# Two-layer transformer and a mixed block on one core: three edits to the order of work around the attention

## The chip, the cores and the metric

The kernel runs on one core of a Trainium2 chip. The metric is device time in microseconds (us) of one execution, the median of several. Engines: PE multiplies matrices, DVE (VectorE) and POOL (GpSimd) do elementwise work, ACT (ScalarE) applies functions and copies, SP issues the DMAs.

## What is computed, cut to what matters

The reference runs a block of two layers on 272 tokens (16 meta tokens and 256 others, 1024 channels), then a second block with routed experts. The change sits in the second layer's attention: 16 query heads of 64 channels, two key/value heads, blocks of 128 queries that see the previous block and their own.

```python
q = (h @ w_q + b_q).reshape(B, L, N_KV_HEADS, GROUP, HEAD_DIM)
...
logits = jnp.einsum('bnqhgd,bnshd->bhgnqs', q, k_blk) * (HEAD_DIM ** -0.5)
logits = jnp.where(valid, logits + bias, -jnp.inf)
m = jnp.maximum(logits.max(axis=-1, keepdims=True), sink)
p = jnp.exp(logits - m)
denom = p.sum(axis=-1, keepdims=True) + jnp.exp(sink - m)
o = jnp.einsum('bhgnqs,bnshd->bnqhgd', (p / denom), v_blk)
return o @ w_o + b_o
```

## The kernel before, in words

Every large matrix product is done in three passes of a reduced format, fp32r, with both factors split into a high and a low part (`mm3`, L1366: high by high, low by high, high by low). A weight piece of 128x2048 comes from HBM into `ring`. ACT makes its high part (`split_hi`, L792), DVE its low part, ring minus high part (`split_lo`, L802); both go to one of four buffer pairs (`wh`/`wl` two of them, `third`, `fourth`). The pieces have one order for the whole program (`NUMBER`), and two counting semaphores, `hi_done` and `lo_done`, say how many are split. `lo_done` is what PE waits for before a product, and what SP waits for before it loads over a ring slot. Four pieces hold w_q (numbers 0 to 3; the key and value weights come between 1 and 2), four hold w_o, then w_gu1 follows.

Each engine runs a program of its own, written out by hand; order within an engine is the order of the code. Around the attention these orders are:

- PE: the products for queries 0 to 3 (a "query" here is a pair of heads, 0 to 7), keys and values; then `scores(0)`, `scores(1)`, `query(4)`, `values()` (three transposes), a wait for `v_ready`; then for u from 0 to 7 `query(5 + u)` (for u below 3), `scores(u + 2)`, for u from 4 the products of w_o's columns 0 and 1 with one pair of heads (`project`), `turn(u)` (transposes of the weights of pair u) and `outputs(u - 1)`. After the loop come the other columns of w_o, c from 0 to 7.
- DVE: `queried(c)` scales a query out of PSUM, `keyed()` the keys (it ends with `kv_ready`, for which `scores(0)` waits), `valued()` the values. `logits(u)` adds the bias and takes the maxima: four instructions that read PSUM and SBUF (L2173), then three on tiles of 128x4 in SBUF (L2181 to L2183), the last of which frees ACT's exponentials. `by_token()` adds the value bias (`v_ready`). `shares(u)` divides: two 128x4 instructions (L2190, L2191) and four on the weights (L2194), for which `turn(u)` waits. `attended_low(u)` (L2199) makes the low part of the output, reading PSUM and SBUF; `project` waits for it. Three low parts of w_o are made by DVE in turns u = 2, 3 and 5.
- ACT: `exps(u + 1)`, `turned(u)` (copies out of PSUM), `attended_high(u - 1)`, and the high parts of w_o: piece 0 ahead of the loop, piece 1 in turn 1, piece 2 in turn 4, piece 3 among the last columns.
- POOL: sums of squares before and after the attention, nothing in between.

`scores(u)` waits for `lg_ready` of `logits(u - 1)`, because the two share PSUM banks. `query(4)` waits for `queried(2)` and `queried(3)`, whose banks it and the next one write over.

Of the kernel before, what the change touches and what calls it, by code (L numbers as in the profile page):

```python
# [5 lines left out]
F32 = mybir.dt.float32  # L6
# [4 lines left out]
ALU = mybir.AluOpType  # L11
# [5 lines left out]
KD = D // P  # L17
# [36 lines left out]
PIECE = 2048  # L54
# [3 lines left out]
FIRST = {}  # L58
# [8 lines left out]
NUMBER = {_piece: _i for _i, _piece in enumerate(SPLIT)}  # L67
FIRST_PIECE = {_name: NUMBER[_name, 0] for _name, _ in SPLIT}
# [84 lines left out]
def bass_two_blocks(nc, a, out):  # L153
# [4 lines left out]
    with ctx:  # L158
# [5 lines left out]
        def sem(name):  # L164
            if name not in sems:
                sems[name] = ctx.enter_context(nc.semaphore(name))
            return sems[name]
# [10 lines left out]
        ring = sb("ring", [P, SLOTS, SLOT])  # L178
# [143 lines left out]
        def tile_at(t):  # L322

            return t % SLOTS, t // SLOTS
# [74 lines left out]
        for part in SPLIT:  # L399
            if part in THIRD:  # L400
                k = 2
            elif part in FOURTH:
                k = 3
            else:
                k, turn_of = turn_of, 1 - turn_of
# [3 lines left out]
        def split_buffer(name, i, j):  # L409

            p = i * 2 + j if type(i) is int else 4 + j
            k = BUFFER[name, p]
            if k >= 2:
                high, low = third if k == 2 else fourth
                return high[:, :], low[:, :]
            return wh[:, k, :], wl[:, k, :]
# [202 lines left out]
        def sum_chunks(pool, name, n):  # L619

            total = sqsum[:, 0:n]
            if SUMMED_BEFORE[name]:
                pool.wait_ge(sem("sq_used"), SUMMED_BEFORE[name])
            pool.wait_ge(sem("sq_ready"), SQ0[name] + 2)
            pool.tensor_tensor(total, square_at(name, 0)[:, 0:n], square_at(name, 1)[:, 0:n], ALU.add).then_inc(sem("sq_summed"), 1)  # L625
            for c in range(2, SUMMED[name]):
                pool.wait_ge(sem("sq_ready"), SQ0[name] + c + 1)
                pool.wait_ge(sem("sq_summed"), sums(name, c - 1))
                pool.tensor_tensor(total, total, square_at(name, c)[:, 0:n], ALU.add).then_inc(sem("sq_summed"), 1)
# [40 lines left out]
            ins.then_inc(sem(done), 1)  # L670


        @block.gpsimd
        def _(pool):
            chain = Chain(pool, "pool_chain")
# [25 lines left out]
            ffn_pool(pool, 0, T)  # L701
            sum_chunks(pool, "ffnpost0", T)
            sum_chunks(pool, "pre1", T)
            sum_chunks(pool, "mixpost1", SEQ)
            sum_chunks(pool, "ffnpre1", SEQ)
            ffn_pool(pool, 1, SEQ)
# [66 lines left out]
            chain(act.activation(r, ps[:, 6, 0:n], ACT.Ln, scale=1.0 / width, bias=EPS))  # L773
            act.activation(r, r, ACT.Exp, scale=-0.5).then_inc(sem("r_ready"), 1)

        def parts_of(name, split, w, size):

            if name != "w_q":
                return [(split[:, 0:size], w)]
            by_pair = split.rearrange("p (k c h n) -> p c k h n", k=KD, h=2, c=2)  # L780
            by_half = w.rearrange("p (k h c n) -> p c k h n", k=KD, h=2, c=2)
            return [(by_pair[:, c], by_half[:, c]) for c in range(2)]

        def split_hi(act, name, slot, rnd, i, j, size):

            if j == 0:
# [4 lines left out]
            for to, src in parts_of(name, high, ring[:, slot, j * size:(j + 1) * size], size):  # L791
                ins = act.activation(to, src, ACT.Copy)  # L792
            ins.then_inc(sem("hi_done"), 1)

        def split_lo(dve, name, slot, rnd, i, j, size):

            piece = NUMBER[name, i * 2 + j] if type(i) is int else i * 2 + (FIRST_PIECE[name] + j)
            dve.wait_ge(sem("hi_done"), piece + 1)
            high, low = split_buffer(name, i, j)
            w = ring[:, slot, j * size:(j + 1) * size]  # L800
            for (to, src), (h, _) in zip(parts_of(name, low, w, size), parts_of(name, high, w, size)):
                ins = dve.tensor_tensor(to, src, h.bitcast(F32), ALU.subtract)  # L802
            ins.then_inc(sem("lo_done"), 1)

        def kv_hi(act):

# [18 lines left out]

        def wo_bank(c):
            return ps[:, (c + 2) % 4, 0:SEQ]

        def halves(name, i, size):
            slot, rnd = tile_at(FIRST[name] + i)  # L830
            return [(slot, rnd, i, j, size) for j in range(2)]

        HEAD_PAIRS = NH // 2

# [505 lines left out]
        def _(pe):  # L1340
# [36 lines left out]
            slot, rnd = tile_at(FIRST["w_pool"])  # L1377
            pe.wait_ge(sem(f"tile_ready{slot}"), 16 * (rnd + 1))
            pw = ring[:, slot, 0:2048].rearrange("p (g k n) -> p g k n", g=4, k=2)
            for c in range(KD):  # L1380
# [4 lines left out]
                for k in range(2):  # L1385
                    ins = mm(ps[:, c % 4, 0:T], pw[:, g, k, c % 2 * P:c % 2 * P + P], pooled[:, 2 * g + k, :],  # L1386
                             start=(k == 0), stop=(k == 1))
# [20 lines left out]
            for c in range(4):  # L1408
                for k in range(KD):
                    pe.wait_ge(sem("x_ready"), KD + k + 1)  # L1410
                    ins = mm(ps[:, c, 0:SEQ], q_weights(c, k)[0], xl[:, k, 0:SEQ], start=False, stop=(k == KD - 1))
# [10 lines left out]
            def query(c):  # L1422

                pe.wait_ge(sem("lo_done"), NUMBER["w_q", c // 2] + 1)
                pe.wait_ge(sem("q_ready"), 4 if c < 6 else c - 1)
                for k in range(KD):
                    ins = mm3(ps[:, 2 + c % 2, 0:SEQ], q_weights(c, k), (xh[:, k, 0:SEQ], xl[:, k, 0:SEQ]), k == 0, k == KD - 1)
                ins.then_inc(sem("q_psum"), 1)
# [9 lines left out]
            def scores(u):  # L1438
                if u >= 4:
                    pe.wait_ge(sem("q_ready"), u + 1)  # L1440
                for j in range(2):
                    rows = slice(j * HD, j * HD + HD)
                    if u:
                        pe.wait_ge(sem("lg_ready"), 4 * (u - 1) + 2 * j + 2)
                    for t in (j, 2 + j):
                        first, n = keys_of(t)
                        ins = mm(score_bank(t)[:, 0:n], qT[rows, u, t // 2 * P:(t // 2 + 1) * P], kT[rows, first:first + n],
                                 start=True, stop=True)
                    ins.then_inc(sem("s_psum"), 1)
# [34 lines left out]

            pe.wait_ge(sem("kv_ready"), 1)
            scores(0)
            scores(1)
            query(4)
            values()
            pe.wait_ge(sem("v_ready"), 2)  # L1490
            for u in range(HEAD_PAIRS):
# [17 lines left out]
            for c in range(4):  # L1509
                for k in range(6, KD):  # L1510
                    ins = project(c, k)
# [3 lines left out]
            for c in range(4, KD):  # L1515
                pe.wait_ge(sem("sq_ready"), SQ0["mixpost1"] + c - 3)
                for k in range(KD):
                    ins = project(c, k)
# [77 lines left out]
            n = Z_HIGH_FIRST  # L1596
# [500 lines left out]
        def _(dve):  # L2097
# [29 lines left out]
            def queried(c):  # L2127

                dve.wait_ge(sem("q_psum"), c + 1)
                chain(dve.tensor_tensor(sq[:, c % 2, 0:SEQ], ps[:, c if c < 4 else 2 + c % 2, 0:SEQ], r[:, N_META:], ALU.mult))  # L2130
                dve.tensor_scalar(qT[:, c, :].rearrange("p (b q) -> p b q", q=P)[:, :, ::-1],
                                  sq[:, c % 2, 0:SEQ].rearrange("p (b q) -> p b q", q=P), query_bias[:, c % 2 * 4 + c // 2:c % 2 * 4 + c // 2 + 1], HD ** -0.5,
                                  ALU.add, ALU.mult).then_inc(sem("q_ready"), 1)

            def keyed():

                dve.wait_ge(sem("kv_psum"), 1)
                chain(dve.tensor_tensor(sq[:, 2, :], ps[:, 4, 0:T], r, ALU.mult))
                dve.tensor_scalar(kT, sq[:, 2, :], key_bias, None, ALU.add).then_inc(sem("kv_ready"), 1)

            def valued():

                dve.wait_ge(sem("kv_psum"), 2)
                dve.tensor_tensor(vT, ps[:, 5, 0:T], r, ALU.mult).then_inc(sem("kv_ready"), 1)

            def by_token():
# [4 lines left out]
                dve.tensor_tensor(vtok[:, 1:NB + 1, :], ps[:, 7, P:3 * P].rearrange("p (b n) -> p b n", b=NB),  # L2151
                                  b_v.unsqueeze(1).to_broadcast([P, NB, P]), ALU.add).then_inc(sem("v_ready"), 1)

            queried(0)
            queried(1)
            split_lo(dve, "w_q", *halves("w_q", 1, PIECE)[0])
            queried(2)
            queried(3)
            keyed()
            split_lo(dve, "w_q", *halves("w_q", 1, PIECE)[1])  # L2160
            dve.wait_ge(sem("tables_loaded"), 64)

            def logits(u):
# [32 lines left out]
            def attended_low(u):  # L2196
                dve.wait_ge(sem("oh_ready"), u + 1)
                o = ps[:, 6 + u % 2, 0:SEQ].rearrange("p (b q) -> p b q", q=P)[:, :, ::-1]
                dve.tensor_tensor(att_l[:, u, :].rearrange("p (b q) -> p b q", q=P), o,  # L2199
                                  att_h[:, u, :].bitcast(F32).rearrange("p (b q) -> p b q", q=P), ALU.subtract)\  # L2200
                   .then_inc(sem("o_ready"), 1)

            logits(0)
            valued()
            logits(1)
            by_token()
            for u in range(HEAD_PAIRS):
                shares(u)
                if u < 4:
                    queried(4 + u)  # L2210
                if u + 2 < HEAD_PAIRS:
                    logits(u + 2)
                if u >= 2:
                    attended_low(u - 2)
                if u in (2, 3, 5):
                    split_lo(dve, "w_o", *[*halves("w_o", 0, PIECE), halves("w_o", 1, PIECE)[0]][(2, 3, 5).index(u)])
            for u in range(HEAD_PAIRS - 2, HEAD_PAIRS):
                attended_low(u)
            split_lo(dve, "w_o", *halves("w_o", 1, PIECE)[1])
            for x in halves("w_gu1", 0, PIECE):  # L2220
                split_lo(dve, "w_gu1", *x)
# [438 lines left out]
```

## Time and profile before

| | |
|---|---|
| runs | 1018.13 us median of 3 (1017.79 to 1020.28) |
| profiled execution | 1017.53 us, its span 1015.8 us |
| busy in the span | PE 94%, DVE 53%, ACT 41%, POOL 20% |
| attention up to the last w_o columns | 257 to 327 us of the span, then PE is busy without a break to 345 |

Times in the trace are from the start of the span. An instruction's row has its start and its duration; a number in brackets is the idle time of the engine before it, and what ended it. The granted clock is a share of PE's full clock of 2.4 GHz; its other level is half of that.

### The profile page before, as it was taken

To read this page: it belongs to the slowest core of one execution; us is meant where nothing else is said; L and a number is where in the kernel's file an instruction comes from. 1 tells how busy PE (TensorE), PEld (TensorE's weight loads), DVE (VectorE), ACT (ScalarE), POOL (GpSimd) and SP (SyncE) were. 2 spreads that over 40 slices of the span, in tenths; PEclk is the share of its full clock that TensorE was granted. 3 is DMA by queue.
4 is the path that set the end of the run, shared out by engine and by line. 5 is a ranking of instruction groups with operands and counts; after the bars stand their busy time and mean duration, and the time that the engine had idled before them with its cause. 6 is when DMAs were issued, how large, how long until landed. Compare 5 with 4: busy or idle time off the path is not lost.

```text
span 1015.8 us, 16586 instructions
## 1 busy us (share of the span) xinstructions
PE 953.5 (94%) x6776; PEld 792.7 (78%) x6776; DVE 537.5 (53%) x931; ACT 415.0 (41%) x691; POOL 202.7 (20%) x261
## 2 busy tenths in 40 slices
PE   4799999999889999999999999988899999999986
PEld 2699999998777899999998999768745545554465
DVE  4765455436966565555448638764632333233266
ACT  4443433435755644344346546743211111111172
POOL 5233333112000433333112412202100000000013
PEclk8799999999998999999999999999899999999998
DMA  7424463448802425533564431118459999999911
GB/s 305 165 85 178 190 227 114 160 164 220 209 31 84 166 85 206 207 139 134 205 226 167 166 127 51 47 54 336 207 216 419 417 420 422 421 422 420 420 66 42
DMA packets 36781, 211.75 MB, mean 208 GB/s; under 512 B 2529, under 2 KB 16113, under 8 KB 17521
## 3 DMA queue, kind: packets, MB, share of 16 engines
q1 hardware_dynamic: 36720, 210.91, 54.5%
q8 instruction: 42, 0.69, 0.3%
q14 instruction: 19, 0.15, 0.0%
HBM read 209.83 MB, written 1.07 MB: 208 GB/s over the span
## 4 chain that ended last, share of the span: by engine, by line
PE 83%; DVE 10%; ACT 3%; POOL 2%; issue 2%; DMA 1%; DVEq 0%; POOLq 0%; ACTq 0%
PE ps L1366 48%; PE ps L1786 11%; PE ps L1800 6%; PE ps L1809 3%; PE ps L1358 2%; DVE mix L1931 2%; PE ps L1758 2%; PE ps L1759 1%; DVE hs L611 1%; PE ps L1293 1%; DVE wl L802 1%; PE ps L1386 1%; PE ps L1301 1%; PE ps L1744 1%; PE ps L1727 1%
## 5 line engine op out<-in xcount | busy, mean ns | idle before, releaser
L802 DVE TENSOR_TENSOR wl<-ring,wh 128x2048 fp32r<-128x2048 f32 (+3 forms) x104 | 205.9, 1981 | 174.6 <-ACT wh L792 174.5
L792 ACT ACTIVATE wh<-ring 128x2048 fp32r<-128x2048 f32 (+3 forms) x104 | 172.3, 1660 | 257.2 <-PE ps L1366 254.9
L1366 PE MATMUL ps<-xh,wh 128*128 128x256 f32 (+3 forms) x600 | 170.0, 283 | 2.3 <-DVE wl L802 1.3
L1366 PE MATMUL ps<-xh,wl 128*128 128x256 f32 (+3 forms) x600 | 168.3, 281 | 0.0
L1366 PE MATMUL ps<-xl,wh 128*128 128x256 f32 (+3 forms) x600 | 168.3, 280 | 0.0
L1366 PEld LDWEIGHTS ps<-xh,wh 128*128 128x128 f32 (+3 forms) x600 | 110.3, 184 | 3.9 <-DVE wl L802 1.5
L1366 PEld LDWEIGHTS ps<-xh,wl 128*128 128x128 f32 (+3 forms) x600 | 110.3, 184 | 0.1
L1366 PEld LDWEIGHTS ps<-xl,wh 128*128 128x128 f32 (+3 forms) x600 | 110.3, 184 | 0.0
L1366 PE MATMUL ps<-acth,wh 128*128 128x272 f32 (+1 forms) x352 | 100.4, 285 | 0.0
L1366 PE MATMUL ps<-acth,wl 128*128 128x272 f32 (+1 forms) x352 | 100.1, 284 | 0.0
L1366 PE MATMUL ps<-actl,wh 128*128 128x272 f32 (+1 forms) x352 | 99.9, 284 | 0.0
L1366 PE MATMUL ps<-xhT,wh 128*128 128x272 f32 x320 | 92.3, 288 | 0.0
L1366 PE MATMUL ps<-xhT,wl 128*128 128x272 f32 x320 | 92.2, 288 | 0.0
L1366 PE MATMUL ps<-xlT,wh 128*128 128x272 f32 x320 | 92.2, 288 | 0.0
L650 POOL TENSOR_TENSOR mix<-mix 128x272 f32<-128x272 f32 (+1 forms) x44 | 36.8, 835 | 156.8 <-DVE mix L1959 141.5
L1366 PEld LDWEIGHTS ps<-acth,wh 128*128 128x128 f32 x352 | 66.4, 189 | 0.0
L2477 DVE TENSOR_TENSOR yl<-ps,yh 128x512 fp32r<-128x512 f32 x32 | 20.6, 686 | 86.3 <-ACT yh L1231 86.3
L1366 PEld LDWEIGHTS ps<-actl,wh 128*128 128x128 f32 x352 | 66.2, 188 | 0.0
L1366 PEld LDWEIGHTS ps<-acth,wl 128*128 128x128 f32 x352 | 66.2, 188 | 0.0
L625 POOL TENSOR_TENSOR sqsum<-mix 128x256 f32<-128x256 f32 (+1 forms) x5 | 4.3, 870 | 280.6 <-ACT mix L767 280.6
L1366 PEld LDWEIGHTS ps<-xhT,wl 128*128 128x128 f32 x320 | 60.3, 188 | 0.0
L1366 PEld LDWEIGHTS ps<-xhT,wh 128*128 128x128 f32 x320 | 60.2, 188 | 0.0
(433 smaller groups left out, 1931.3 us busy)
## 6 DMA issues: line engine op xcount, KB each, us to landing
wring<-in_w_eg SPq DMA_DIRECT2D x32, 2048.0 KB, 13.4
ring<-in_w_gu SPq DMA_DIRECT2D x22, 2048.0 KB, 7.5
wring<-in_w_ed SPq DMA_DIRECT2D x16, 2048.0 KB, 12.0
ring<-in_w_dn SPq DMA_DIRECT2D x16, 1408.0 KB, 6.0
ring<-in_w_z SPq DMA_DIRECT2D x7, 2048.0 KB, 7.7
ring<-in_w_out SPq DMA_DIRECT2D x4, 1152.0 KB, 5.1
ring<-in_w_q SPq DMA_DIRECT2D x8, 512.0 KB, 6.3
ring<-in_w_o SPq DMA_DIRECT2D x8, 512.0 KB, 15.6
```

Of the source, the lines that this page charges most:

```text
L611: eng.tensor_tensor(hs[:, c, cols], hs[:, c, cols], mix[:, c, 0:n], ALU.add).then_inc(hs_add(c), 1)
L650: pool.tensor_tensor(mix[:, 6 + j, 0:n], mix[:, 2 + j, 0:n], mix[:, 4 + j, 0:n], ALU.mult)\
L792: ins = act.activation(to, src, ACT.Copy)
L802: ins = dve.tensor_tensor(to, src, h.bitcast(F32), ALU.subtract)
L1358: mm(ps[:, 6, 0:n], ones[0:rows, :], src, start=first, stop=(c == last)).then_inc(sem("sq_used"), summed if c < summed else 1)
L1366: ins = mm(o, p, q, start=first and n == 0, stop=last and n == 2)
L1758: mm(out, h2h[:, k, at], select[:, k, :], start=(k == 0), stop=False)
L1786: ins = mm(ps[rows, 4, :], x[:, k, rows], chunk(slot)[:, j, i * 512:(i + 1) * 512], start=(k == 0), stop=(k == KD - 1))
L1800: ins = mm(ps[rows, 6 + i, :], heT[:, k, rows], chunk(slot)[:, j, k * D + i * 512:k * D + (i + 1) * 512], start=(k == 0), stop=(k == 1))
L1809: ins = mm(ps[:, c // 2, c % 2 * SEQ:(c % 2 + 1) * SEQ], y[:, c * P:(c + 1) * P], weights, start=False, stop=last and y is parts[-1], skip ...
L1931: return dve.scalar_tensor_tensor(dst, src, V(name, c), r, ALU.mult, ALU.mult)
L2477: dve.tensor_tensor(yl[:, i * 512:(i + 1) * 512], ps[:, 6 + i, :], yh[:, i * 512:(i + 1) * 512].bitcast(F32), ALU.subtract).then_inc(sem(" ...
```

## The change

Three edits. (1) On DVE the low part of w_q's piece 2 moves ahead of `queried(0)`, and `keyed()` ahead of `queried(2)`; the low part of piece 3 moves behind `logits(0)` and `valued()`. (2) On PE `query(4)` moves between `scores(0)` and `scores(1)`. (3) The low parts of w_o's pieces 0, 1 and 2 are made by POOL, which first waits until all pieces before w_o are done; DVE makes that of piece 3 after a wait for POOL's last. `halves`, `parts_of` and `split_lo` move up in the file without a change.

```diff
@@ POOL's program
             sum_chunks(pool, "pre1", T)
+            pool.wait_ge(sem("lo_done"), NUMBER["w_o", 0])
+            for x in [*halves("w_o", 0, PIECE), halves("w_o", 1, PIECE)[0]]:
+                split_lo(pool, "w_o", *x)
             sum_chunks(pool, "mixpost1", SEQ)
@@ PE's program
             pe.wait_ge(sem("kv_ready"), 1)
             scores(0)
+            query(4)
             scores(1)
-            query(4)
             values()
@@ DVE's program
+            split_lo(dve, "w_q", *halves("w_q", 1, PIECE)[0])
             queried(0)
             queried(1)
-            split_lo(dve, "w_q", *halves("w_q", 1, PIECE)[0])
+            keyed()
             queried(2)
             queried(3)
-            keyed()
-            split_lo(dve, "w_q", *halves("w_q", 1, PIECE)[1])
             dve.wait_ge(sem("tables_loaded"), 64)
...
             logits(0)
             valued()
+            split_lo(dve, "w_q", *halves("w_q", 1, PIECE)[1])
             logits(1)
             by_token()
...
                 if u >= 2:
                     attended_low(u - 2)
-                if u in (2, 3, 5):
-                    split_lo(dve, "w_o", *[*halves("w_o", 0, PIECE), halves("w_o", 1, PIECE)[0]][(2, 3, 5).index(u)])
             for u in range(HEAD_PAIRS - 2, HEAD_PAIRS):
                 attended_low(u)
+            dve.wait_ge(sem("lo_done"), NUMBER["w_o", 3])
             split_lo(dve, "w_o", *halves("w_o", 1, PIECE)[1])
```

## Rows read from the trace of the kernel before

**Rows 1.** PE by stretch: us, PE busy (instructions), granted clock, DMA share, GB/s.

```profile
276.80:281.20 4.40, 4.40 (x26) 0.64 0.98 417
299.30:305.30 6.00, 3.78 (x34) 0.88 0.00 0
315.70:321.20 5.50, 3.79 (x25) 0.69 0.00 0
257.00:327.00 70.00, 61.00 (x494) 0.93 0.39 108
```

**Rows 2.** Timeline of PE: start, duration, instruction, idle before it.

```profile
272.40 0.40 PE L1447 MATMUL ps<-work 64*128 64x144 f32 x2 [1.69 <-DVE work L2139]
275.24 0.39 PE L1447 MATMUL ps<-work 64*128 64x144 f32 x1 [1.88 <-DVE small L2173]
282.32 0.39 PE L1366 MATMUL ps<-xh,third_h 128*128 128x256 f32 x1 [0.70 <-DVE work L2151]
285.33 0.95 PE L1447 MATMUL ps<-work 64*128 64x144 f32 x8
302.43 0.33 PE L1459 MATMUL ps<-cst,work 128*128 128x128 f32 x1 [2.22 <-DVE work L2194]
317.41 0.44 PE L1459 MATMUL ps<-cst,work 128*128 128x128 f32 x1 [1.74 <-DVE work L2194]
```

**Rows 3.** Timeline of DVE around the queries, keys and first logits.

```profile
266.36 0.42 DVE L2130 TENSOR_TENSOR sq<-ps,rstd 128x256 f32<-128x256 f32 x1
271.99 0.36 DVE L2139 TENSOR_SCALAR work<-sq,small 128x272 f32<-128x272 f32 x1
275.79 0.17 DVE L2181 TENSOR_TENSOR small<-small,row 128x4 f32<-128x4 f32 x1
276.14 0.43 DVE L2144 TENSOR_TENSOR work<-ps,rstd 128x272 f32<-128x272 f32 x1
```

**Rows 4.** Timeline of DVE, a low part of w_o and what follows.

```profile
299.22 2.28 DVE L802 TENSOR_TENSOR wl<-ring,wh 128x2048 fp32r<-128x2048 f32 x1
301.42 0.16 DVE L2190 TENSOR_TENSOR small<-small 128x4 f32<-128x4 f32 x1
```

**Rows 5.** The page, DMA issues: KB each, us to landing.

```profile
ring<-in_w_gu SPq DMA_DIRECT2D x22, 2048.0 KB, 7.5
```

**Rows 6.** Timeline of POOL after the attention.

```profile
333.82 0.75 POOL L625 TENSOR_TENSOR sqsum<-sq 128x256 f32<-128x256 f32 x1 [76.82 <-ACT sq L767]
```

**Rows 7.** Groups by form on POOL: busy, mean ns; idle before.

```profile
L656 POOL TENSOR_TENSOR actl<-mix,acth 128x272 f32 x22 | 17.1, 775 | 3.7 <-POOL acth L653 3.7
L694 POOL TENSOR_TENSOR sgw<-sgw,cst 128x512 f32<-128x512 f32 x1 | 1.3, 1263 | 9.2 <-DMA sgw<-in_sgw 9.2
```

**Rows 8.** Timelines of POOL and DVE at three places where both work.

```profile
17.40 1.28 POOL L603 TENSOR_TENSOR work<-work 128x512 f32<-128x512 f32 x1
17.47 1.51 DVE L1931 SCALAR_TENSOR_TENSOR work<-hs,vec,rstd 128x272 f32<-128x272 f32 x1
...
565.14 2.29 DVE L802 TENSOR_TENSOR wl<-ring,wh 128x2048 fp32r<-128x2048 f32 x1 [3.46 <-ACT wh L792]
565.45 2.58 POOL L723 TENSOR_TENSOR work<-work,rstd 128x256 f32<-128x256 f32 x1 [9.69 <-ACT work L1033]
...
1003.79 0.72 POOL L641 TENSOR_TENSOR sqsum<-sqsum,sq 128x256 f32<-128x256 f32 x1
1003.84 0.43 DVE L2507 TENSOR_TENSOR mix<-ps,rstd 128x256 f32<-128x256 f32 x1 [0.82 <-PE ps L1366]
```

**Rows 9.** Timeline of DVE, the second row of group 8's kind, undisturbed.

```profile
248.03 0.50 DVE L1931 SCALAR_TENSOR_TENSOR mix<-mix,vec,rstd 128x272 f32<-128x272 f32 x1 [2.15 <-ACT rstd L774]
```

**Rows 10.** Timeline of ACT, two high parts of w_o.

```profile
293.57 1.91 ACT L792 ACTIVATE third_h<-ring 128x2048 fp32r<-128x2048 f32 x1
...
311.26 1.91 ACT L792 ACTIVATE wh<-ring 128x2048 fp32r<-128x2048 f32 x1
```

More of the change, by code:

```diff
@@ L670, in conv, with halves, parts_of, split_lo @@
             ins.then_inc(sem(done), 1)
+        def halves(name, i, size):
+            slot, rnd = tile_at(FIRST[name] + i)
+            return [(slot, rnd, i, j, size) for j in range(2)]
+        def parts_of(name, split, w, size):
+            if name != "w_q":
+                return [(split[:, 0:size], w)]
+            by_pair = split.rearrange("p (k c h n) -> p c k h n", k=KD, h=2, c=2)
+            by_half = w.rearrange("p (k h c n) -> p c k h n", k=KD, h=2, c=2)
+            return [(by_pair[:, c], by_half[:, c]) for c in range(2)]
+        def split_lo(dve, name, slot, rnd, i, j, size):
+            piece = NUMBER[name, i * 2 + j] if type(i) is int else i * 2 + (FIRST_PIECE[name] + j)
+            dve.wait_ge(sem("hi_done"), piece + 1)
+            high, low = split_buffer(name, i, j)
+            w = ring[:, slot, j * size:(j + 1) * size]
+            for (to, src), (h, _) in zip(parts_of(name, low, w, size), parts_of(name, high, w, size)):
+                ins = dve.tensor_tensor(to, src, h.bitcast(F32), ALU.subtract)
+            ins.then_inc(sem("lo_done"), 1)
         @block.gpsimd
@@ L774, in rsqrt @@
             act.activation(r, r, ACT.Exp, scale=-0.5).then_inc(sem("r_ready"), 1)
[L776 to L782, printed above, removed]
         def split_hi(act, name, slot, rnd, i, j, size):
@@ L793, in split_hi @@
             ins.then_inc(sem("hi_done"), 1)
[L795 to L803, printed above, removed]
         def kv_hi(act):
@@ L827, in wo_bank @@
             return ps[:, (c + 2) % 4, 0:SEQ]
-        def halves(name, i, size):
-            slot, rnd = tile_at(FIRST[name] + i)
-            return [(slot, rnd, i, j, size) for j in range(2)]
         HEAD_PAIRS = NH // 2
```

## The prediction

> **What bounds the kernel now.** PE is busy 94% of the span, so I looked for the stretches where it is not. PE's windows show one around the attention: of 70.0 us from 257 to 327 it is busy 61.0, and its granted clock is 0.93 [rows 1]. So 9.0 us are idle time and another 4.9 (70.0 x 0.07) are half-speed time; after 327 PE runs densely again, so whatever reaches the end of `outputs(7)` earlier ends the kernel earlier by as much. Next, PE's own timeline names the stalls [rows 2]: 1.69 us ahead of `scores(0)` (the keys, L2139), 1.88 ahead of `scores(1)` (the end of `logits(0)`'s use of the banks), 0.70 ahead of `query(5)` (`by_token`), 2.22 ahead of `turn(3)` and 1.74 ahead of `turn(6)`, the last two for `shares`. Each is a wait for DVE. The reader is to see that the stalls cost twice: behind the first pair the clock is 0.64 for 4.40 us of `query(4)`, 1.6 us lost; behind the stall of 2.22 it is 0.88 over 6.0 us, 0.7 lost; at `turn(6)` 0.69 over 5.5, 1.7 lost [rows 1]. DVE's timeline then shows what stands ahead of the waits.
>
> **Edit 1, keys earlier.** DVE is free for the queries at 266.36 and done with the keys at 272.35 [rows 3]; in these 6.0 us lie four `queried`, a split (2.2 us, from one start to the next [rows 4]) and `keyed` (0.85), so a `queried` is 0.73. Two of them leave the path: keys at 270.9. The split of w_q's piece 2 stands ahead either way, and its high part comes from ACT's earlier work. PE ends the values' product at 270.71 (272.40 less 1.69), so `scores(0)` goes at 270.95 and ends at 271.9 (0.95 [rows 2]).
>
> **Edit 2, `query(4)` in between.** It needs `queried(3)`, whose end stays at 272.35. It takes 3.0 us at full clock (282.32 to 285.33, `query(5)`) and covers `logits(0)`: PE ends it at 275.35, `scores(1)` at 276.3, the transposes at 276.8. On DVE, without the split of piece 3 (2.2), `logits(0)` ends at 273.95 instead of 276.14 [rows 3]; `valued` 0.35, the split 2.2: DVE turns to `logits(1)` at 276.5. Its four PSUM reads take 1.3 (1.65 in all, less the 0.35 from 275.79 to 276.14 [rows 3]): 277.8. If nothing else came, 0.35 for the small instructions and 0.7 for `by_token` [rows 2] would start `query(5)` at 278.8, 3.5 us earlier than 282.32. The load of w_gu1 over piece 3's slot is issued by SP behind that split, 1.9 us later than now; it lands in 7.5 us [rows 5] and ACT reads it some 50 us later, so it costs nothing.
>
> **Edit 3, low parts by POOL.** POOL has nothing from 257 to 333.82 [rows 6], so its own time is free. DVE loses three splits, 6.6 us. The price of one on POOL is not in the trace: 0.775 us for 272 elements, 1.263 for 512 [rows 7]. The slope gives 0.775 + 1776 x 0.00203 = 4.4 us; in proportion to the smaller one it would be 5.8. I take 4.4, because the two rows show a fixed part; 5.8 is kept as the upper end, and 4.0 as the lower for a slope measured on one instruction. `project` needs piece 0 some 20 us after it is ready and piece 1 and 2 in the columns behind 327, so that POOL is slow costs PE nothing directly.
>
> It costs through DVE. Three places show both at work [rows 8]. A POOL instruction of two SBUF inputs runs 17.40 to 18.68; DVE's L1931 (two SBUF inputs) that starts at 17.47 takes 1.51 instead of 0.50 [rows 9] and ends 0.3 after POOL's. The other way round, POOL's 256 elements that start 0.31 into a split of DVE take 2.58 us and end 0.6 after it. But L2507, which reads PSUM and SBUF, takes 0.43 in the middle of a POOL instruction. So I read: an instruction with two SBUF inputs waits until the other engine's is over, one that reads PSUM doesn't. The Trainium skill ("SBUF — State Buffer", section "Who interferes with whom") states this for any length: the pair of ports is held for the whole instruction, and the second to come fully blocks. The sum below is by whole holds, as the rows of up to 2.3 us show; the first rival is the sum if a hold of 4.4 us doesn't happen. The same skill's "GPSIMD Engine Reference" (section "Performance versus the Vector engine") gives 4497 ns for a two-input operation of 2048 elements, no run here shows it; with it the sum would be 0.3 us higher.
>
> Piece 0: POOL waits for w_q's last split, 276.5, and so starts exactly when DVE turns to `logits(1)`. The four PSUM reads pass, the 128x4 instructions of L2181 to L2183 (two SBUF inputs) meet POOL's hold at 277.8 and wait until 276.6 + 4.4 = 281.0. Behind them on DVE are `by_token` and `shares(0)`; PE waits for the first: 281.0 + 0.35 + 0.7 = 282.05, against 282.32. Of the 3.5 us, 0.3 are left. And PE is now idle in one piece, 276.8 to 282.05, 5.2 us, where before two stalls with 3.6 us were followed by a loss of 1.6. I expect 1.6 to 3.2 lost in `query(5)` and `query(6)`, and take 1.9. Turns 0 to 2, which PE paces, are then 1.6 late (1.9 - 0.3).
>
> Piece 1: ACT makes its high part 1.6 late, 295.2 to 297.1 [rows 10]; POOL holds 297.1 to 301.5. The small instructions of `logits(4)` come inside this and wait; then 0.35, `attended_low` 0.33, and 1.0 of `shares(3)` (301.42 to 302.43 [rows 2, 4]): `turn(3)` at 303.2, 0.8 late. The wait replaces the split.
>
> Piece 2: from `turn(3)` to ACT's next high part are 8.8 us now (302.43 to 311.26 [rows 2, 10]), DVE's second split in them; 2.2 less, 0.3 more where PE becomes the pace: 6.9, so 310.1, ready 312.0. POOL holds to 316.4, and again the small instructions (here of `logits(7)`) come into it; 0.35 + 0.33 + 1.0: `turn(6)` at 318.1 against 317.41. The stall ahead of it is longer than now, the slow clock behind it the same.
>
> **Sum: -0.3 + 1.9 (clock) - 0.8 (turn 3) - 2.0 (turn 4) + 1.9 (turn 6) = +0.7 us.** The profiled execution (1017.53, span 1015.8) would be 1018.2; the median of the runs is 0.6 above it, so 1018.8. Each microsecond on POOL's 4.4 comes three times. Own range: POOL at 4.0 and the clock at 1.6 give -0.8, POOL at 4.8 and 3.2 give +3.2: 1017 to 1021.5.
>
> **Rivals.** (a) DVE isn't held. Then `query(5)` gains 3.5, `turn(3)` its stall of 2.2 and the 0.7 of clock, `turn(4)` 0.6 by the same reckoning, `turn(6)` 1.7 and 1.7: 10.4 us, 1007.7. For it: no row has a hold of 4 us. Against: none of the rows shows a hold end early. 0.13. (b) Only the long ones are held, the 128x4 ones slip through; no row shows one beside a two-input POOL instruction. `query(5)` at -3.5; POOL holds 292.0 to 296.4, `shares(3)` comes at 295.7 and waits 0.7, `turn(3)` at 297.4, -5.0; third high part ready at 305.9, hold to 310.3, `turn(6)` at 311.3: -6.1 us, 1012.0. 0.14. (c) The other side: POOL's price is nearer 5.8. With three times the difference the sum is +4.9, 1023.0; it is slower by over 0.3% from 5.2 us on. For it the proportion, against it the two rows' slope. 0.14. (d) `logits`' reads of PSUM, a custom instruction with its second input in SBUF, are held too: 1.2 us more behind piece 0 and 1.0 more behind piece 1, some of it kept: +2.9, 1021.7. L2507 speaks against it. 0.09. My forecast: 0.50.
>
> **The numbers.** About 0.3%, 3.1 us, is what a measurement of this kernel can tell from no change. Faster: (a), (b): 0.27. Slower: (c) above 5.2 us and a part of (d), 0.18. The rest, 0.55. The range leaves out (a) and the end of (c): 1010.5 to 1022.5.
>
> **What would show it.** `scores(0)` near 271, `query(4)` at a full clock near 272.4; three POOL splits of 4.4 us; at the first, L2181 behind `logits(1)` at 3 us instead of 0.17, ending with POOL's; PE idle near 5 us ahead of `query(5)` and a low clock behind it; `turn(3)` and `turn(6)` each released by a DVE that had waited for POOL. I am wrong if L2181 is short there, if POOL's splits are not near 4.4, or if the clock stays at 1.00 after the long idle time.

## The result, and the profile after

The change makes the kernel slower: 1022.82 us median of 20 runs against 1019.15 (20 runs), ratio 1.0034 (1.0024 to 1.0044), that is 3.5 us. I had said 1018.8 against 1018.13, or +0.7. So 1.0 us of the 4.0 between 1018.8 and 1022.82 is the kernel before, whose median went from 1018.13 (3 runs) to 1019.15. The profiled execution of the change has a span of 1019.5 us, against 1015.8.

PE's timeline of the kernel after: `scores(0)`, `query(4)`, `query(5)`, `turn(3)` and `turn(6)`.

```profile
270.34 0.95 PE L1450 MATMUL ps<-work 64*128 64x144 f32 x8 [0.37 <-DVE work L2142]
271.88 0.35 PE L1369 MATMUL ps<-xh,third_h 128*128 128x256 f32 x1 [0.58 <-DVE work L2134]
281.39 0.58 PE L1369 MATMUL ps<-xh,third_h 128*128 128x256 f32 x1 [5.16 <-DVE work L2154]
302.02 0.33 PE L1462 MATMUL ps<-cst,work 128*128 128x128 f32 x1 [1.45 <-DVE work L2196]
316.72 0.47 PE L1462 MATMUL ps<-cst,work 128*128 128x128 f32 x1 [3.67 <-DVE work L2196]
```

Of the two stalls of 1.69 and 1.88 us, 0.37 ahead of `scores(0)` and 0.58 ahead of `query(4)` are left. `query(4)` starts at 271.88, `query(5)` waits 5.16 us, `turn(3)` 1.45 instead of 2.22, and `turn(6)` 3.67 instead of 1.74.

The timeline of POOL in the kernel after, from its last sum of squares before the attention to the first behind it. I use the distance of the starts of these two rows as the length of the attention in every run below.

```profile
254.32 1.92 POOL L629 TENSOR_TENSOR sqsum<-sqsum,mix 128x272 f32<-128x272 f32 x2 [1.24 <-ACT mix L792]
276.03 4.50 POOL L692 TENSOR_TENSOR wl<-ring,wh 128x2048 fp32r<-128x2048 f32 x1 [19.79 <-DVE wl L692]
295.92 4.54 POOL L692 TENSOR_TENSOR third_l<-ring,third_h 128x2048 fp32r<-128x2048 f32 x1 [15.39 <-ACT third_h L809]
310.63 4.54 POOL L692 TENSOR_TENSOR wl<-ring,wh 128x2048 fp32r<-128x2048 f32 x1 [10.17 <-ACT wh L809]
335.43 0.74 POOL L625 TENSOR_TENSOR sqsum<-sq 128x256 f32<-128x256 f32 x1 [20.26 <-ACT sq L792]
```

It is 81.11 us (335.43 less 254.32); before, 78.74 (333.82 in [rows 6] less 255.08, where the same row stands in the timeline of the kernel before). DVE's timeline of the kernel after shows what each of POOL's three splits does, at the first 128x4 instruction of `logits(1)`, `logits(4)` and `logits(7)` (0.17 us in [rows 3]):

```profile
277.13 3.42 DVE L2183 TENSOR_TENSOR small<-small,row 128x4 f32<-128x4 f32 x1
...
298.44 0.42 DVE L2175 CUSTOM_DVE_ANT_0 work<-ps,work 128x256 f32<-128x256 f32 x1
...
298.90 1.59 DVE L2183 TENSOR_TENSOR small<-small,row 128x4 f32<-128x4 f32 x1
...
310.91 4.28 DVE L2183 TENSOR_TENSOR small<-small,row 128x4 f32<-128x4 f32 x1
```

Each ends where POOL's split ends (276.03 + 4.50 = 280.53; 295.92 + 4.54 = 300.46; 315.17), though it works on four elements per partition. The next one, at 280.58, takes 0.16 again. The row with PSUM as its first input, at 298.44, lies within POOL's second split and takes its usual 0.42.

PE's windows from `turn(6)` to POOL's first sum, in the order: the kernel before, the kernel before in a second profiled execution (a run below), the kernel after, and the kernel after in its second. Columns as in [rows 1].

```profile
317.40:333.80 16.40, 16.39 (x141) 0.90 0.00 1
```

```profile
317.50:332.40 14.90, 14.82 (x141) 1.00 0.00 1
```

```profile
316.70:335.40 18.70, 18.68 (x141) 0.77 0.00 1
```

```profile
316.60:335.30 18.70, 18.67 (x140) 0.77 0.00 1
```

The same work without a break takes 14.9 us at a full clock, 16.4 at 0.90 and 18.7 at 0.77. Up to `turn(6)` the two kernels are equal (62.3 us from the first POOL row before, 62.4 after). What the change adds to the attention comes behind it.

The attention is not the whole difference of the two spans: 3.7 us are 0.8 less ahead of it, 2.4 more in it and 2.1 more behind it, where the code is the same. PE's windows from 700 to 760 us, before and after, show a lower clock there:

```profile
700.00:760.00 60.00, 52.73 (x294) 0.94 0.60 245
```

```profile
700.00:760.00 60.00, 52.90 (x289) 0.89 0.56 228
```

From POOL's sum at 702.70 to the next, at 980.36, are 277.7 us before; in the change 279.9 (704.55 to 984.41). Of the runs below, the second execution of the kernel before, e4 and e9 have 277.6 to 277.7, all others 279.6 to 281.8. Since two variants of the change have the short time and e1 and e6, without POOL, the long one, it doesn't go with the edits. What sets it is open.

### The profile page after: what moved, and what is told of

Read it like the earlier page. It is cut to its first block, busy times and chain, and to the rows that moved or that the text cites. A ratio compares the mean times of both kernels' runs of the same rounds, so it can differ in the third digit from the quotient of the medians.

```text
span 1019.5 us, 16588 instructions
## 1 busy us (share of the span) xinstructions
PE 952.9 (93%) x6776; PEld 791.7 (78%) x6776; DVE 540.2 (53%) x928; ACT 415.7 (41%) x691; POOL 216.8 (21%) x264
## 4 chain that ended last, share of the span: by engine, by line
PE 79%; DVE 13%; ACT 3%; POOL 2%; issue 2%; DMA 1%; POOLq 0%; DVEq 0%; ACTq 0%
PE ps L1369 46%; PE ps L1789 11%; PE ps L1803 6%; PE ps L1812 3%; DVE mix L1934 2%; PE ps L1761 2%; PE ps L1361 2%; DVE hs L611 2%; PE ps L1762 2%; DVE wl L692 1%; DVE small L2183 1%; PE ps L1304 1%; PE ps L1747 1%; DVE work L2175 1%; PE ps L1389 1%
## 5 line engine op out<-in xcount | busy, mean ns | idle before, releaser
L692 DVE TENSOR_TENSOR wl<-ring,wh 128x2048 fp32r<-128x2048 f32 (+3 forms) x102 | 201.5, 1977 | 174.6 <-ACT wh L809 174.5
```

## The experiments

All ran beside the kernel before. "Attention" is the distance defined above, from one profiled execution each; "rest" is what the span has behind it, where no run differs in its code. What lies ahead of the attention takes 254.1 to 255.3 us in every one. A single execution can lie far from the median of its kernel: that of e4 is the fastest of 12 runs (1014.84 us, median 1019.04), that of e8 the slowest of 6 (1026.22, median 1023.02). A difference "by the runs" between two variants is that of their ratios, each known to 1.0 to 3.0 us either way.

| run | ratio to before (interval) | attention | rest |
|---|---|---|---|
| before; again | 1 | 78.7; 77.2 | 682.0; 683.3 |
| change; again | 1.0034 (1.0024 to 1.0044) | 81.1; 81.3 | 684.1; 684.0 |
| e1 edits 1 and 2 alone | 0.9974 (0.9959 to 0.9990) | 75.7 | 686.7 |
| e2 edit 3 alone | 1.0020 (1.0006 to 1.0033) | 81.4 | 684.1 |
| e3 filler at both stalls | 0.9982 (0.9969 to 0.9994) | 76.0 | 686.4 |
| e7 filler at `turn(6)` | 1.0007 (0.9993 to 1.0022) | 77.6 | 684.6 |
| e9 filler at `query(5)` | 1.0012 (0.9996 to 1.0027) | 79.0 | 683.7 |
| e4 first split behind `shares(0)` | 0.9996 (0.9984 to 1.0008) | 75.7 | 682.2 |
| e10 third split behind `shares(7)` | 0.9987 (0.9973 to 1.0001) | 74.8 | 685.2 |
| e8 POOL's splits in halves | 1.0039 (1.0026 to 1.0053) | 81.6 | 688.1 |
| e5 all three where DVE is free of them | 0.9940 (0.9924 to 0.9956) | 69.8 | 689.1 |
| e6 the three on DVE, in its idle times | 0.9902 (0.9872 to 0.9931) | 69.8 | 683.7 |

**e1 and e2: which edit costs.** e1 is the change without its lines on POOL, with DVE's three splits back at u = 2, 3 and 5. e2 has only those lines.

> Edits 1 and 2 alone; DVE makes the three low parts of w_o where it did before. Theory (POOL's splits hold DVE, and the idle time this leaves on PE costs clock): query(5) starts near 278, 3.5 us earlier than before, the four stalls behind it are as before, and so the kernel is 3 to 4 us faster than before, near 0.9965. Rival (the move of query(4) is what costs, since PE has nothing behind it but the wait for the values): PE idle of 4 us or more ahead of query(5) and low clock there with no POOL at work, time 1 to 4 us above before.

> Edit 3 alone. Theory: POOL starts behind w_q's last split, now ahead of logits(0); its three 128x4 instructions are held some 3.4 us, query(4) covers that on PE, and query(5) starts within 0.3 us of before. turn(3) 0.7 earlier, turn(6) 0.7 earlier but behind a longer stall, with up to 2.3 us more at half clock: 0 to +2 us against before. Rival (the three edits do harm only together): 3 us or more faster, since DVE is rid of 6.6 us.

The orders on DVE and PE are worth 2.7 us by the runs (3 to 4 forecast) and 3.0 or 1.5 by the attention, against the first or the second execution of the kernel before; `query(5)` starts at 278.16, behind 1.89 us of idle time, so the rival on edit 2 falls. POOL alone costs 2.0 us, with a stall of 3.66 ahead of `turn(6)` and the clock at 0.77 behind it, as in the change. The rival that edit 3 is good by itself falls too. Its time is at the upper end of the forecast, but the starts that I gave were missed: counted from POOL's last sum, `query(5)` comes 1.3 us later than before (forecast within 0.3), `turn(3)` 0.5 and `turn(6)` 0.3 later (forecast 0.7 earlier each). `scores(1)` takes 2.27 us there instead of 1.62, and in `query(4)` the clock is 0.50 from 277 to 280 us.

**e3, e7, e9: what the idle time costs in clock.** `stay_busy` issues bf16 products whose result nobody reads.

```diff
             values()
+            stay_busy(pe, 4, 21)                  # e3, e9
             pe.wait_ge(sem("v_ready"), 2)
...
+                if u == 6:                        # e3, e7
+                    pe.wait_ge(sem("pt_ready"), 12)
+                    stay_busy(pe, 4, 14)
                 turn(u)
```

> The change, and PE multiplies filler (bf16, 512 columns, nothing is read of it) into free banks during its two long idle times: 21 behind the transposes of the values, 14 ahead of turn(6). Theory (the clock behind the idle times is the part that I sized too small): the granted clock stays 1.00 behind both, 1.4 us come back at query(5) and up to 4 behind turn(6), so the kernel is 4 to 5 us faster than the change and 0 to 2 us faster than before. Rival (the loss lies elsewhere, behind the attention): within 1.5 us of the change.

> The change, with filler on PE ahead of turn(6) only. Theory (my sum left out the longer half-clock time behind the longer stall at turn(6)): the low clock behind query(5) stays, that behind turn(6) goes; 2.5 to 4 us faster than the change, that is 0 to 1 us above before. Rival (the stall ahead of query(5) is the larger part): under 1.5 us faster than the change.

> The change, with filler on PE ahead of query(5) only. The attention is counted from POOL's last sum before it to POOL's first sum after it: 78.7 us before, 81.1 in the change, 76.0 with filler at both places, 77.6 with filler at turn(6) only. Theory (the two low clocks cost independently): 79.3 to 79.9, 1.2 to 1.8 below the change. Rival (the filler only shifts the low clock to a later stretch): within 0.5 of the change's 81.1.

Up to the filler nothing moves: counted from POOL's last sum, `query(5)` starts at 27.1 us in e3 and e9 as in the change, and `turn(6)` at 62.7 in e7, against 62.4. The clock differs, with what follows from it, and the attention falls from 81.2 to 77.6 with filler at `turn(6)`, to 79.0 at `query(5)`, to 76.0 at both: 3.6, 2.2 and 5.2 us. By the runs, the change's 3.5 us become 0.7, 1.2 and -1.8. The 79.0 of e9 is outside the 79.3 to 79.9 that I expected: only 1.3 of its 2.2 us are won ahead of `turn(6)`, the other 0.8 behind it, where the clock is 0.81 over 17.9 us behind the same stall of 3.67. From `turn(6)` on, the run with filler there shows a full clock again:

```profile
317.50:332.20 14.70, 14.70 (x140) 1.00 0.00 1
```

**e4 and e10: one hold at a time.**

```diff
             pool.wait_ge(sem("lo_done"), NUMBER["w_o", 0])
+            pool.wait_ge(sem("p_ready"), 4)                # e4: shares(0) is done
...
+            pool.wait_ge(sem("p_ready"), 4 * HEAD_PAIRS)   # e10, ahead of piece 2: shares(7) is done
```

> The change, with POOL's first split held back until shares(0) is done, so that it runs where DVE waits for PE. Theory: L2183 (the 128x4 instruction) is 0.17 us in logits(1), query(5) starts near 278.3 instead of 281.4 of the change and at a full clock; 4 to 5 us faster than the change, about 1 us faster than before; turn(6) still has its long stall and the low clock. Rival (the first hold is cheap, the one at turn(6) is all that matters): under 2 us faster than the change.

> The change, with POOL's third split alone held back until shares(7) is done. Theory (the third hold costs its own 3.3 us of stall ahead of turn(6) and the low clock behind it): attention 75 to 76 us, 5 to 6 below the change, turn(6) behind an idle time under 0.7 us. Rival (ACT's high part and exponentials, not POOL's hold, set turn(6)): idle time ahead of turn(6) above 2 us, attention above 78.

Without the first hold the attention is 5.5 us shorter than in the change, without the third 6.4 (the stall ahead of `turn(6)` is 0.43). By the runs it is 3.9 and 4.8 us (4 to 5 forecast for e4). Against the kernel before, neither is told from no change. Only 3.1 of e4's 5.5 us lie ahead of `turn(6)`. The rest is the clock behind it, in PE's windows of e4:

```profile
314.50:330.90 16.40, 16.38 (x141) 0.90 0.00 1
```

The stall ahead of `turn(6)` is 3.66 us here, as in the change, and what follows is as in the kernel before with its stall of 1.74. So the length of the stall alone does not set the clock behind it.

In e4 the hold lands elsewhere, on an instruction with a single SBUF input (0.35 us elsewhere), which my reading of [rows 8] says nothing of, and PE waits 1.27 us for it ahead of `query(6)`; POOL's split runs from 280.40 to 284.94. DVE's timeline of e4:

```profile
280.64 4.45 DVE L2135 TENSOR_SCALAR work<-sq,small 128x256 f32<-128x256 f32 x1
```

**e8: how a hold is dealt out.** POOL makes each low part as two instructions of 128x1024.

> The change, with each of POOL's three splits as two instructions of 1024 elements. Theory (a hold lasts as long as the instruction, and POOL's next one starts as soon as DVE's small one is through): in logits(1) L2181's kind waits about 1.3 us for the first half, the next small instruction 2.3 us for the second; DVE is free as late as in the change, and the time is within 1 us of it. Rival (between the halves DVE gets all three small ones through): query(5) starts 2 us earlier than in the change, and the kernel is 3 to 5 us faster than it.

Timelines of POOL and of DVE in e8:

```profile
276.49 4.64 POOL L694 TENSOR_TENSOR wl<-ring,wh 128x1024 fp32r<-128x1024 f32 x2 [19.78 <-DVE wl L696]
```

```profile
277.61 1.25 DVE L2187 TENSOR_TENSOR small<-small,row 128x4 f32<-128x4 f32 x1
278.89 2.26 DVE L2188 TENSOR_TENSOR small<-row,small 128x4 f32<-128x4 f32 x1
```

One small instruction gets through between the halves, the next waits for the whole second half. The sum is 3.5 us, against 3.42 in the change, and nothing is gained. This agrees with the Trainium skill ("SBUF — State Buffer", section "Who interferes with whom"), by which a hold lasts one instruction.

**e5 and e6: a version that beats both.** e5 has the waits of e4, and of e10 for pieces 1 and 2. e6 has edits 1 and 2 and nothing on POOL:

```diff
                 if u < 4:
                     queried(4 + u)
+                if u == 0:
+                    split_lo(dve, "w_o", *halves("w_o", 0, PIECE)[0])
...
-            for u in range(HEAD_PAIRS - 2, HEAD_PAIRS):
-                attended_low(u)
+            split_lo(dve, "w_o", *halves("w_o", 0, PIECE)[1])
+            attended_low(HEAD_PAIRS - 2)
+            split_lo(dve, "w_o", *halves("w_o", 1, PIECE)[0])
+            attended_low(HEAD_PAIRS - 1)
```

> As the run with POOL's first split behind shares(0), and pieces 1 and 2 held back as well, until shares(7) is done; DVE then has only instructions that read PSUM (attended_low). Theory: no 128x4 instruction of logits(4) and logits(7) is held, turn(3) and turn(6) follow shares without a long stall, no half clock from 257 to 327, the attention 8 to 10 us shorter than before; 0.991 to 0.993. Rival (the columns 2 to 5 of w_o now wait for POOL's late pieces, which need 9.1 us behind shares(7)): a stall of 1 us or more near 318 to 325 on PE, ratio above 0.995.

> Edits 1 and 2, nothing on POOL: DVE makes piece 0 in turn 0 behind queried(4), piece 1 behind attended_low(5) and piece 2 behind attended_low(6), where it waited for ACT before. Theory (what the splits cost is their place, not DVE's busy time): as good as POOL with late pieces, within 1.5 us of it, since a split is 2.2 us here and 4.5 there; 0.991 to 0.993. Rival (DVE's load is the limit, and POOL is needed): 2 us or more behind the run with late pieces on POOL.

Both attentions are 69.8 us, 9 below the first execution of the kernel before and 7 below the second, with no stall above 0.5 us between `turn(3)` and POOL's first sum. DVE's timeline of e6 shows two of the splits where DVE waited for ACT:

```profile
313.01 0.42 DVE L2198 TENSOR_TENSOR attended<-ps,attended 128x256 fp32r<-128x256 f32 x1
313.34 2.28 DVE L692 TENSOR_TENSOR third_l<-ring,third_h 128x2048 fp32r<-128x2048 f32 x1
...
315.88 2.28 DVE L692 TENSOR_TENSOR wl<-ring,wh 128x2048 fp32r<-128x2048 f32 x1
```

e6 is 10.0 us faster than before (0.9902). e5, with the same attention, gives only 6.1. I had expected 0.991 to 0.993 for both, and the two within 1.5 us of each other. PE's window of e5 and that of the kernel before show where the rest went:

```profile
650.00:760.00 110.00, 97.88 (x538) 0.86 0.49 191
```

```profile
650.00:760.00 110.00, 97.34 (x573) 0.95 0.46 181
```

The clock is lower in e5 between 650 and 760 us (0.86 against 0.95), in code that all runs share. Whether that is chance of these runs or follows from when that stage begins isn't settled.

**The last two runs: the kernels once more, one profiled execution each.**

> The change once more, for a second profile. Theory: attention 81.1 within 0.7; what the profiled execution of the change was longer beyond 2.4 us lies behind the attention, where the granted clock differs from execution to execution. Rival: the part behind the attention is 684 us again and the attention differs.

> The kernel before once more, for a second profile. Theory: attention 78.7 within 0.7; the part behind it differs from the first profile's 682.0 by 1 us or more, with the granted clock between 650 and 750 us. Rival: 682.0 again within 0.5, so that the 684.1 of the change is an effect of the change.

The change repeats itself to 0.2 us, in the attention and in the rest. The kernel before doesn't: its attention is 77.2 this time, since behind the same stall of 1.74 us ahead of `turn(6)` the clock stays at 1.00. My expectation of 78.7 within 0.7 missed, and the miss is instructive: against this execution the change costs 3.9 to 4.1 us in the attention, against the first 2.4 to 2.6; the runs' median says 3.5. The rest was 683.3 against 682.0, so it too differs between executions of one kernel; but the 2.2 us between the two sums above are there in both executions of the change (279.9) and in neither of the kernel before (277.7), though two variants of the change, e4 and e9, are without them.

## Why the prediction was wrong

- **Keys earlier, `query(4)` in between: right.** `query(4)` starts at 271.88, which is 272.6 on the scale of before (POOL's last sum is 0.76 earlier here), and 272.35 was forecast.
- **POOL's price: right.** 4.4 us forecast, 4.50 to 4.54 measured; rival (c), 5.8, is gone. The 4497 ns of the Trainium skill ("GPSIMD Engine Reference", section "Performance versus the Vector engine") agrees with the trace.
- **The holds: right.** All three met the 128x4 instructions (3.42, 1.59, 4.28 us), so rivals (a) and (b) are gone; the reads of PSUM passed, so (d) is gone. Counted from POOL's last sum, `query(5)` starts 0.2 us earlier than before (forecast 0.3), `turn(3)` 0.35 later (forecast 0.8), `turn(6)` 0.1 later (forecast 0.7).
- **Who is held: right as far as it went.** My reading names instructions with two SBUF inputs and those that read PSUM. e4's 4.45 us show one with a single SBUF input held too. Nothing in the sum hangs on it.
- **The clock behind `query(5)`: the right mechanism, 0.6 too much.** 1.9 us forecast. `query(5)` takes 4.35 us (281.39 to 285.74) instead of 3.0, so 1.3 were lost, and e9 wins 1.3 back ahead of `turn(6)`. That is why `turn(6)` came only 0.1 late, not 0.7.
- **The clock behind `turn(6)`: the step that failed.** I wrote: "The stall ahead of it is longer than now, the slow clock behind it the same." The sum put the difference at nothing, without a reason. The stall was longer, 3.67 us against 1.74, and the clock behind it was not the same: 0.77 over 18.7 us in both executions, against 0.90 over 16.4 or 1.00 over 14.9. The term of `turn(6)` should have had 2.3 to 3.8 us more, and with it the sum is 3.0 to 4.5 (2.4 to 3.9 with the measured 1.3 at `query(5)`), where the runs say 3.5. How close that comes is in part luck, since the sum has nothing of the 0.7 to 2.1 us that the profiled executions differ by behind the attention. e7 takes this clock away and gets 3.6 us of attention back, e10 takes the hold away and gets 6.4 back. Why the clock was low for so long stays open: behind a stall of 3.6 to 3.7 us the same work took 18.7 to 18.9 us in the change, e2 and e8, but 17.9 in e9 and 16.4 in e4. I had also read the 1.7 us lost at `turn(6)` before as a fixed part of that stall, from one execution; in the second it was not there.
- **The chances.** The mechanism that I gave 0.50 is the one that ran. Its own range, 1017 to 1021.5, was too low by the failed term and by the 1.0 us of the kernel before; the slower side, 0.18, got its chance from (c) and (d), which both proved false.

## What to carry to other kernels

Before work moves to an idle POOL, look at what DVE does in those microseconds: a split of 4.5 us held even a four-element instruction until it ended, and cutting it in two didn't help. In the attention what decided was the place, not the engine: with the same edits 1 and 2, it is 81.1 us with the splits in one place and 69.8 in the two others, on POOL or on DVE. And when a stall of PE doubles, give the clock behind it a range and not a number: here it cost 1.5 to 4.0 us behind stalls of the same length, and one execution of the old kernel doesn't say what the short stall cost on the average.

## What the runs showed of the hardware that I had not expected

- A stall of 1.74 us ahead of `turn(6)` was followed by a lowered clock in one execution of the kernel before and not in the other; one of 3.6 to 3.7 us was in all six executions that have it, but at 0.77 in four (both of the change, e2, e8), at 0.81 in e9 and at 0.90 in e4.
- The part of the kernel behind the attention, the same code in all runs, took 682.0 to 689.1 us, the longest with a granted clock of 0.86 between 650 and 760 us. One stretch of it took 277.6 to 277.7 us in four executions and 279.6 to 281.8 in ten. Differences of a few microseconds between two single profiles need the part named in which they arise.
- A DVE instruction with one SBUF input was held as well: 128x256, SBUF to SBUF, took 4.45 us instead of 0.35 beside POOL's split in e4.
- A held DVE instruction shows as one that takes long (4.28 us for 128x4), not as idle time of DVE, so the list of waits in the attention of the change names POOL nowhere as what DVE waited for.
